# Block attention by pairs of heads, and VectorE's order around it

## The reference, cut to what matters

```python
s_own = jnp.einsum('bhqd,bhkd->bhqk', q_c, k_own) + bias_own
s_own = jnp.where(own_pos[None, :] <= q_pos[:, None], s_own, -jnp.inf)
probs = jax.nn.softmax(logits, axis=-1)
out = jnp.einsum('bhqk,bhkd->bhqd', p_own, v_own)
# the time mix, per head and token
y = ((y - mean) * rsqrt(var + LNX_EPS)) * ln_g + ln_b
bonus = jnp.sum(r * k * r_k, axis=-1, keepdims=True) * v
y = (y + bonus) * g
```

## Time and profile before

| what | value |
|---|---|
| median of 3 runs | 2366.2 us (2364.02 to 2369.61) |
| the profiled execution's own time | 2367.74 us |
| its span in the profile | 2366.0 us |
| TensorE matmuls busy | 97% of the span |
| VectorE, ScalarE busy | 46%, 18% |
| mean granted clock | 0.99 |

### The profile page before, as it was taken

The page is one execution under the profiler, slowest core; times in us unless marked ns, Lnnn a source line. Parts: engine busy times, 40 slices in busy tenths (PEclk is TensorE's granted clock), DMA queues, the critical chain, the costliest instruction groups (busy, mean ns, idle before and its releaser), DMA issues. The chain is left out here.

```text
span 2366.0 us, 28968 instructions
## 1 busy us (share of the span) xinstructions
PE 2303.2 (97%) x12084; PEld 1559.8 (66%) x12084; DVE 1088.2 (46%) x2045; ACT 423.8 (18%) x838; POOL 48.1 (2%) x77
## 2 busy tenths in 40 slices
PE   6999999999999989999999999999999999999998
PEld 4778854444444468758767768748857866776873
DVE  2788331111111176742453356666664155335665
ACT  1123321111111121100322211101101131221110
POOL 1000000000000010000000000000000000000000
PEclk8999999999999999999999999999999999999999
DMA  9656569999999965443230544436544342044541
GB/s 385 257 213 262 192 211 360 422 422 422 422 422 422 410 191 163 178 160 128 103 135 2 178 152 159 162 120 218 178 152 172 104 160 90 15 165 151 176 157 59
DMA packets 175997, 499.74 MB, mean 211 GB/s; under 512 B 6904, under 2 KB 99336, under 8 KB 146064
## 3 DMA queue, kind: packets, MB, share of 16 engines
q1 hardware_dynamic: 171920, 481.23, 54.2%
q0 software_dynamic: 3824, 16.43, 2.3%
q10 hardware_dynamic: 144, 0.52, 0.1%
HBM read 491.34 MB, written 6.82 MB: 211 GB/s over the span
## 5 line engine op out<-in xcount | busy, mean ns | idle before, releaser
L2120 PE MATMUL bank<-Tw,Sx 128*128 128x256 f32 x960 | 213.8, 379 | 0.0
L2120 PEld LDWEIGHTS bank<-Tw,Sx 128*128 128x128 f32 x960 | 179.4, 190 | 22.6
L2208 PE MATMUL bank<-xT,ring 128*128 128x256 f32 x704 | 152.6, 379 | 0.0
L863 PE MATMUL bank<-xT,ring 128*128 128x256 f32 x640 | 143.7, 385 | 2.8 <-ACT xT L281 2.8
L2208 PEld LDWEIGHTS bank<-xT,ring 128*128 128x128 f32 x704 | 133.6, 190 | 17.8
L2120 PE MATMUL bank<-ring,xT 128*128 128x256 f32 x640 | 144.7, 379 | 0.0
L863 PEld LDWEIGHTS bank<-xT,ring 128*128 128x128 f32 x640 | 122.8, 193 | 21.8 <-ACT xT L281 2.9
L2120 PEld LDWEIGHTS bank<-ring,xT 128*128 128x128 f32 x640 | 121.7, 190 | 18.1 <-issue 1.9
L1426 PE MATMUL bank<-ring,xg 128*64 128x512 f32 x512 | 113.9, 593 | 5.1 <-DMA ring<-in_w 5.1
L1463 PE MATMUL bank<-ring,hTg 128*64 128x512 f32 x512 | 113.4, 595 | 0.0
L1426 PE MATMUL bank<-more,xg 128*64 128x512 f32 x512 | 112.6, 592 | 0.0
(11 more groups left out here) (519 smaller groups left out, 3589.1 us busy)
## 6 DMA issues: line engine op xcount, KB each, us to landing
ring<-in_w SPq DMA_DIRECT2D x128, 1024.0 KB, 17.4
ring<-in_ffn_w_in SPq DMA_DIRECT2D x88, 1024.0 KB, 7.7
ring<-in_first_pieces SPq DMA_DIRECT2D x33, 2048.0 KB, 12.1
more<-in_w SPq DMA_DIRECT2D x64, 1024.0 KB, 17.1
ring<-in_ffn_w_out SPq DMA_DIRECT2D x20, 2048.0 KB, 7.9
ring<-in_w_mix_in SPq DMA_DIRECT2D x12, 2048.0 KB, 7.9
ring<-in_xattn_w_kv SPq DMA_DIRECT2D x8, 2048.0 KB, 8.1
ring<-in_w_mix_out SPq DMA_DIRECT2D x4, 2048.0 KB, 9.7
```

The costliest lines, as they stand in the source:

```text
L863: last = nc.tensor.matmul(b[:, c * SEQ:(c + 1) * SEQ], w[:, k, m * P:(m + 1) * P], xT[:, k, :], start=(k == 0), stop=(k == KD - 1))
L2120: last = nc.tensor.matmul(bank[BANK_OF[name]][:, 0:SEQ], lhs(k), rhs(k), start=(k == 0), stop=(k == 3))
L2208: last = nc.tensor.matmul(b[:, c * SEQ:(c + 1) * SEQ], w[:, k, col:col + P], xT[:, k, :], start=(k == 0), stop=(k == KD - 1))
```

## The change

TensorE's three steps take a pair p of heads and issue the products of the two halves alternately: the two short scores, then the two long ones; six transposes; the two long values, then the two short ones. A pair's turning waits for both divisions, a pair's scores stand behind it, and its values behind a filler. ScalarE copies both turned heads, then takes the next pair's two exponentials, then `take_kv`, which stands once for each pair. VectorE does both logits of a pair, then both divisions. At the start, VectorE takes the bonus right behind the two logits, ahead of both divisions, and both divisions ahead of the four maskings; ScalarE does `expo(1)` ahead of `take_kv(3)`. In the loop, the second half of a product 1 or 3 is masked between logits and divisions, the inverse's start follows the divisions, and the first half of product 3 comes behind that. The diff, the lines added (those taken out are in the kernel above):

```diff
...
+                def half(h):
+                    return slice((h % 2) * HD, (h % 2) * HD + HD)
+                def scores(p):
+                    if p:
+                        pe.wait_ge(mb_sb, l * NH + 2 * p)
+                    heads = (2 * p, 2 * p + 1)
+                    for h in heads:
+                        nc.tensor.matmul(bank[4 + h % 2][:, 0:P], qm[half(h), p, 0:P], km[half(h), p, 0:P],
+                                         start=True, stop=True)
+                    for h in heads:
+                        nc.tensor.matmul(bank[4 + h % 2][:, P:384], qm[half(h), p, P:SEQ], km[half(h), p, :],
+                                         start=True, stop=True).then_inc(at_s, 1)
+                def turned(p):
+                    pe.wait_ge(at_p, l * N_AT + (2 * p + 2))
+                    if p:
+                        pe.wait_ge(at_tc, l * N_AT + 2 * p)
+                    for h in (2 * p, 2 * p + 1):
+                        for c in range(3):
+                            last = nc.tensor.transpose(bank[6 + h % 2][:, c * P:(c + 1) * P],
+                                                       sm[:, h % 2, c * P:(c + 1) * P], eye)
+                        last.then_inc(at_t, 1)
+                def values(p):
+                    pe.wait_ge(at_tc, l * N_AT + (2 * p + 2))
+                    heads = (2 * p, 2 * p + 1)
+                    o = bank[2 + p // 2][:, (p % 2) * SEQ:(p % 2 + 1) * SEQ]
+                    for h in heads:
+                        nc.tensor.matmul(o[half(h), :], vm[:, 0, h * HD:(h + 1) * HD], pmT[:, h % 2, 0:SEQ],
+                                         start=True, stop=False)
+                    for h in heads:
+                        nc.tensor.matmul(o[half(h), P:SEQ], vm[:, 1, h * HD:(h + 1) * HD], pmT[:, h % 2, SEQ:384],
+                                         start=False, stop=True).then_inc(at_o, 1)
...
+                quarters = [range(n, n + 2) for n in range(0, KD, 2)]
+                    fill = [((6 + p // 2, quarters[2 * (p % 2)]), (6 + p // 2, quarters[2 * (p % 2) + 1]))
+                            for p in range(NH // 2)]
+                    fill = [((4 + p, range(0, 4)), (4 + p, range(4, KD))) for p in range(NH // 2)]
+                for p in range(NH // 2):
+                    if p == 0:
+                    turned(p)
+                    if p < NH // 2 - 1:
+                        scores(p + 1)
+                    if 0 < p < 3:
+                        mats(l, 2 * p - 1, (1,))
+                    cross_kv(l, *fill[p][0])
+                    if p == 2:
+                    values(p)
+                    cross_kv(l, *fill[p][1])
+                    if p < 2:
+                        mats(l, 2 * p + 1, (0,))
...
+                expo(1)
+                for p in range(NH // 2):
+                    for h in (2 * p, 2 * p + 1):
+                        act.wait_ge(at_t, l * N_AT + (h + 1))
+                        if p:
+                            act.wait_ge(at_o, l * N_AT + (h - 1))
+                        nc.scalar.activation(pmT[:, h % 2, :], bank[6 + h % 2][:, 0:384], ACT.Copy).then_inc(at_tc, 1)
+                    if p < NH // 2 - 1:
+                        expo(2 * p + 2)
+                        expo(2 * p + 3)
+                    if l:
+                        take_kv(4 + p)
+                    elif p % 2:
+                        take_kv(6 + p // 2)
+                    if p % 2:
+                        act.wait_ge(at_o, l * N_AT + (2 * p + 2))
+                        m = 4 + 2 * (p // 2)
+                        nc.scalar.activation(flat(xT[:, m:m + 2, :]), bank[2 + p // 2][:, :],
...
+                logits(1)
+                for n in range(2):
+                    dve.wait_ge(heads_psum, l * N_HEADS + (n + 3))
+                    last = nc.vector.tensor_tensor(flat(bon[:, 2 * n:2 * n + 2, :]), bank[6 + n][:, :],
+                                                   flat(pT[:, 8 + 2 * n:10 + 2 * n, :]), ALU.mult)
+                last.then_inc(bonus_ready, 1)
+                probs(0)
+                probs(1)
+                dve.wait_ge(fac_ready, l + 1)
+                dve.wait_ge(bonus_ready, l + 1)
+                for ch in range(2):
+                    for e in range(2):
+                        diagonal(2 * ch, e, Lt, C_LOWER)
+                for p in range(NH // 2 - 1):
+                    dve.wait_ge(at_t, l * N_AT + (2 * p + 2))
+                    logits(2 * p + 2)
+                    logits(2 * p + 3)
+                    if p:
+                        diagonal(2 * p - 1, 1, X, C_LEV)
+                    probs(2 * p + 2)
+                    probs(2 * p + 3)
+                    if p:
+                        inverse_start(p - 1)
+                    if p < 2:
+                        diagonal(2 * p + 1, 0, X, C_LEV)
```

More of the change, by code:

```diff
@@ L2355, in moba_attention @@
                 pe.wait_ge(lora_act, (l + 1) * N_LORA)
                 scores(0)
-                scores(1)
                 cross_kv(l, 1)
@@ L2364, in moba_attention @@
                 cross_kv(l, 3)
-                low, high = range(0, 4), range(4, KD)
+                quarters = [range(n, n + 2) for n in range(0, KD, 2)]
                 if l == 0:
-                    fill = {0: [(6, low)], 1: [(6, range(4, 6))], 2: [(6, range(6, KD))], 3: [(7, range(0, 2))],
-                            4: [(7, range(2, 4))], 5: [(7, range(4, 6))], 6: [(7, range(6, KD))]}
-                else:
[L2371 to L2374, removed]
+                    fill = [((6 + p // 2, quarters[2 * (p % 2)]), (6 + p // 2, quarters[2 * (p % 2) + 1]))
+                            for p in range(NH // 2)]
+                else:
+                    fill = [((4 + p, range(0, 4)), (4 + p, range(4, KD))) for p in range(NH // 2)]
+                for p in range(NH // 2):
+                    if p == 0:
                         pe.wait_ge(mat_dve, l * N_MDVE + 4)
[L2376 to L2379, removed]
-                        pe.wait_ge(mat_dve, l * N_MDVE + 8)
[L2381 to L2385, removed]
+                    turned(p)
[5 more added lines that the diff above has]
+                    if p == 2:
+                        pe.wait_ge(mat_dve, l * N_MDVE + 8)
+                    values(p)
+                    cross_kv(l, *fill[p][1])
+                    if p < 2:
+                        mats(l, 2 * p + 1, (0,))
             def rwkv_heads(l):
@@ L3202, in mixer @@
                 logits(0)
[L3203 to L3224, removed]
```

## The result

The changed kernel takes 2343.48 us (median of 4, 2340.30 to 2344.35); the kernel before, run beside it, 2367.9 us (median of 4, 2364.02 to 2371.62). The ratio on record is 0.9903, 95% interval 0.9891 to 0.9914 (it isn't the quotient of the two medians, which is 0.9897). The profiled executions took 2344.35 us and 2367.74 us, their spans are 2342.5 and 2366.0: 23.5 us less.

A forecast was written before the change was run, and what follows sets the result against it. TensorE's matmuls, filling 97% of the span, were taken to bound the kernel. 12.0 us less work, 4.9 bonus wait, 4.2 other waits and 1.7 clock made 22.8 off 2367.7, so 2345 us; own range 2340 to 2350, full 2340 to 2353.

The forecast's parts named there:

- scores, gain a layer: TensorE's scores: six heads at 0.85 us become three pairs at 0.87, 2.5 us a layer less.
- values: TensorE's values: a pair's column halves overlap, 0.80 us a pair against 0.79 a head, 3.1 us a layer less.
- turnings: TensorE's transposes: six together cost 0.8 us against 0.96 for two threes, 0.6 us a layer less.
- waits inside the heads: TensorE's waits for ScalarE's copies (3.8 us) and a division (0.9) go, one of 0.5 comes: net 4.2 us.
- bonus: VectorE's bonus ahead of the divisions: TensorE's 2.45 us wait for it goes in both layers, 4.9 us.
- new wait of 0.5 us at the third pair: Layer 0: the third pair's values wait for bank 3 until VectorE's last masking, 0.5 us, bounds 0 to 1.2.
- margin of 1.0 us at the first turning: VectorE's four maskings end at 1181.2, TensorE reaches the first turning at 1182.2: 1.0 us to spare.
- margins of 1.4, 2.0 and 1.3 us: Layer 0, rounds p = 0, 1, 2: time by which the pair's divisions are ready before TensorE's next turning.
- clock term of 1.7 us: Layer 1's filler ahead of the first turning: half-clock loss behind the idle goes with it, 1.7 us, with a doubt.
- Half-clock stretches in the new order: Listed sign of a wrong forecast: TensorE running partly at 1.2 GHz instead of 2.4 in the changed kernel.
- third rival: Saving given back later, at a transfer or ScalarE's last copies: at most 2367 us, no change; chance 0.03.
- second and fourth rival: Second: VectorE and ScalarE late, 2350 to 2353 us, chance 0.13. Fourth: changing halves drains the array, 2369 us, chance 0.02.

The follow-up runs named there:

- e7: Changed kernel with VectorE's loop masking placed between the two logits of a pair instead of behind them: 2341.55 us, 0.9903.
- e8: Changed kernel with the two maxima of each head taken three times, the extra results unused: 2350.43 us, 0.9943.
- e3: Changed kernel with the values of a pair's two heads on either side of the second filler, one head at a time: 2349.27 us, 0.9935.
- e2: Changed kernel with VectorE's bonus put back behind the division of head 0: 2347.60 us, 0.9933.
- e12: Kernel before with only SyncE's second load of the cross attention's query weights issued later: 2361.97 us, 0.9985.
- e1: Kernel before with only VectorE's bonus moved ahead of the first division, heads still one by one: 2358.23 us, 0.9970.
- e10: Changed kernel with the last filler of each layer's loop ahead of the last pair's values: 2343.53 us, 0.9907.
- e6: Changed kernel with both first divisions behind the four maskings, the bonus still ahead of both: 2344.02 us, 0.9909.
- e5: Changed kernel with each pair's scores and values kept together but issued head by head instead of alternating: 2343.02 us, 0.9907.
- e9: Changed kernel with SyncE's second 2 MB load of query weights held until behind the first product of the inverse's last step: 2337.63 us, 0.9883.

## Why the prediction was right

The forecast was 2345 us, measured 2343.5. Its base was the profiled execution of 2367.7 us: it took 22.8 us off, and the two profiles differ by 23.5. By its own steps, layer 0 against the profile after:

| step | predicted | measured |
|---|---|---|
| scores, gain a layer | 2.5 | 2.7 (5.10 to 0.86 + 0.76 + 0.77) |
| values | 3.1 | 3.1 (6.32 to 4 x 0.80) |
| turnings | 0.6 | 0.8 (3.84 to 0.75 + 0.81 + 0.80 + 0.66) |
| masked products | 0 | 0.2 (two of four at 0.98) |
| fillers | - 0.2 | - 0.2 (15.02 to 15.19) |
| waits inside the heads | 2.3 | 2.3 (2.85 to 0.56) |
| bonus | 2.45 | 2.45 |

- Layer 0's heads were to take 29 to 30 us and took 28.5; layer 1's 42 to 43 and took 41.6. By the table the difference is 0.2 us each at the scores, the masked products and the turnings. The first two are halves of rows that stand next to each other, which I had priced as if full-width work stood between; the third is mostly the last pair's turning, 0.66 us between two fillers.
- The small error of the sum hides two larger ones that cancel: the stages gained 17.5 us where 16.2 were forecast, and 1.2 were lost outside them.
- The new wait of 0.5 us at the third pair is there, 0.56, for the masking named; e7 takes it away by the order alone.
- The margin of 1.0 us at the first turning was 1.0. The margins of 1.4, 2.0 and 1.3 us were 1.1, 1.8 and 1.2; e8 used them up: its new waits came to 6.7 us against the 7.3 worked out from these margins.
- That a pair of values costs what one head's did came from the earlier trace rows; e3 and the profile after bear it out, at 0.80. The rule weighed against it ("TensorE: Matmul & The Clock Gate", Part 3, The mechanism, of the Trainium skill: weight loads overlap matmuls in flight only when the row group differs) isn't borne out for column halves here. The prediction took that sentence by itself; the same section also lets a load run ahead when it goes to the background weight buffer, so it speaks less clearly against the term than was said.
- The clock term of 1.7 us was in this pair of profiles, but e2 and e12 show the same idle twice each without it. As a term of the change it was luck. "Half-clock stretches in the new order" was also named as a sign of being wrong, and there is one, 0.73 over 1973.7 to 1980; but the kernel before has its like behind the same stall (0.80 over 1991.6 to 2000), so the change didn't bring it.
- The third rival happened on a small scale: 1.2 us came back as longer stalls inside the inverse. With one head at a time they were 2.2 and 1.6 us in all (before, e1), with pairs and the early load 2.8 to 3.5 in all nine profiles. Why pairs lengthen them stays open; e10 speaks against the load's later start as the reason for most of it. I had looked for waits for a DMA in the stage and for late stores, and not at the stalls that no engine's work ends, 2.2 us in the kernel before.
- The second and fourth rival did not come about: no turning waits for a division in the profile after, and pairs of scores and values take 0.76 to 0.86 us.
- The sum over the profiles: 9.0 + 8.5 + 4.9 + 1.7 - 1.2 = 22.9 of the 23.5 us; of the remaining 0.6, 0.4 are shorter waits for transfers far from the stage (L795 16.6 to 16.4, L1426 5.1 to 4.9).
- VectorE's divisions ahead of the maskings, which the change makes a point of, are worth nothing (e6), nor is the alternating order (e5).

## What to carry to other kernels

Small products that use one half of the array should stand next to products of the other half; here how they alternate made no difference, and a filler between them did. Look for the same pattern elsewhere in the trace before estimating: one row of the time mix showed that a pair overlaps, 0.65 us, and with the 0.15 us of switching estimated from one head alone it gave the 0.80 measured. When the chain is one engine's, check which stalls carry no releaser, and try moving a large load away from them before rebuilding the schedule: here one wait on SyncE gave a quarter of what the whole change did.

## What was not expected of the hardware

- With a 2 MB load issued right behind the stage, beside a store, TensorE stood still for 1.4 and 2.0 us inside work that by the profile waits for no engine and no transfer; issuing the load some 40 us later removed both (e9), and the kernel before's 0.3 and 1.9 us likewise (e12).
- The same idle of 2.4 us was followed by a clock of 0.80 over 8.7 us once, and by 1.00 five times; one of 2.75 us by 0.54 over 3 us (e8).
- One head's products in half of the rows take 0.85 us next to full-width products and 0.76 next to other half-row products: a switch between shapes seems to cost about 0.1 us (the masked product next to them is 0.1 shorter too).
